# Between router and first expert group: another order of the first gather, of four identity products and of the overflow flag

## The reference

```
h = rms_norm(x, moe_norm_w)
gl = h @ w_rg + b_rg                       # group logits
gp = softmax(gl); gi = top_k(gl, 1)        # one group per token
el = (h @ w_re + b_re)[chosen group]       # 8 logits
top_v, top_i = top_k(el, 2); top_w = softmax(top_v) * g_w
comb = weight of each of 32 experts, zero for all but two
out = sum over experts e of
      (silu(h @ w_gate[e]) * (h @ w_up[e]) * comb[:, e]) @ w_down[e]
x = x + out
```

## Time and profile before

| | us |
|---|---|
| three runs: median (lowest to highest) | 846.97 (846.54 to 847.56) |
| profiled execution, its own time | 844.72 |
| its span, first to last instruction | 842.9 |
| mean granted TensorE clock, share of full | 0.966 |
| TensorE matmul busy | 760.5 (90%) |
| VectorE busy / ScalarE busy | 459.2 (54%) / 325.0 (39%) |
| moved by DMA | 190.25 MB, mean 226 GB/s |

### The profile page before, as it was taken

How to read it: one execution, slowest core, us unless ns; L and a number is a source line. 1 busy time by engine, 2 the same in 40 slices (tenths; PEclk the granted TensorE clock), 3 DMA queues, 4 the chain that set the end, 5 groups by cost and what they waited for, 6 DMA issues and landing times.

```text
span 842.9 us, 11017 instructions
## 1 busy us (share of the span) xinstructions
PE 760.5 (90%) x4618; PEld 573.6 (68%) x4618; DVE 459.2 (54%) x813; ACT 325.0 (39%) x482; POOL 17.8 (2%) x14
## 2 busy tenths in 40 slices
PE   4999999999999997988799896779999999999898
PEld 4978877788778875555445542337999865678676
DVE  5778955547756755132142121028687786754653
ACT  5555446535464423111011010037755541267521
POOL 0000000000000000000000000001100020000000
PEclk9999999999999997999899898789999999999999
DMA  9555543333467596699999999875463734243301
GB/s 317 172 199 199 200 150 101 100 101 101 149 244 277 191 425 260 213 422 420 421 421 420 419 422 391 338 265 185 146 228 94 255 130 149 101 150 100 100 1 51
DMA packets 62578, 190.25 MB, mean 226 GB/s; under 512 B 7417, under 2 KB 11771, under 8 KB 50044
## 3 DMA queue, kind: packets, MB, share of 16 engines
q1 hardware_dynamic: 60750, 184.70, 58.6%
q10 hardware_dynamic: 1774, 4.79, 1.8%
HBM read 188.43 MB, written 1.05 MB: 225 GB/s over the span
## 4 chain that ended last, share of the span: by engine, by line
PE 59%; DMA 16%; DVE 13%; ACT 8%; issue 2%; POOL 1%; SPq 0%; ACTq 0%; DVEq 0%; POOLq 0%
PE pb L500 56%; DMA raw<-in_w_exp_up 7%; DVE WL L1705 4%; DMA WHo<-in_w_exp_up 4%; ACT WH L1209 4%; PE pb L509 3%; DMA WLo<-in_w_exp_up 3%; DMA raw<-in_w_exp_gate 2%; ACT arena L1365 1%; DMA X<-in_x 1%; DVE cv_ L1811 1%; DVE arena L1970 1%; POOL small L2587 1%; ACT arena L1237 0%; DVE arena L2016 0%
## 5 line engine op out<-in xcount | busy, mean ns | idle before, releaser
L1705 DVE TENSOR_TENSOR WL<-raw,WH 128x2048 fp32r<-128x2048 f32 (+5 forms) x80 | 173.4, 2177 | 98.2 <-ACT WH L1209 98.1
L1209 ACT ACTIVATE WH<-raw 128x2048 fp32r<-128x2048 f32 (+5 forms) x80 | 144.9, 1822 | 99.4 <-PE pb L500 89.9
L500 PE MATMUL pb<-WH,HTh 128*128 128x512 f32 (+2 forms) x384 | 156.0, 406 | 13.6 <-DVE HTl L1735 3.4
L500 PE MATMUL pb<-WL,HTh 128*128 128x512 f32 (+2 forms) x384 | 148.3, 386 | 0.0
L500 PE MATMUL pb<-WH,HTl 128*128 128x512 f32 (+2 forms) x384 | 148.0, 386 | 0.0
L500 PEld LDWEIGHTS pb<-WH,HTh 128*128 128x128 f32 x384 | 72.7, 189 | 33.7 <-DVE WL L1705 6.4
L500 PEld LDWEIGHTS pb<-WL,HTh 128*128 128x128 f32 x384 | 72.5, 189 | 14.4
L500 PEld LDWEIGHTS pb<-WH,HTl 128*128 128x128 f32 x384 | 72.8, 190 | 12.9 <-issue 1.0
L500 PE MATMUL pb<-arena 128*32 128x256 f32 (+6 forms) x268 | 64.0, 466 | 7.4 <-DMA arena<-in_w_exp_up 4.8
L500 PE MATMUL pb<-WH,arenao 128*128 128x512 f32 x192 | 59.6, 392 | 1.2 <-DVE arenao L1739 1.2
L2244 DVE TENSOR_TENSOR rt_<-rt_,pb 128x256 f32<-128x256 f32 x8 | 3.4, 421 | 98.9 <-ACT rt_ L1480 98.9
(11 more groups left out here) (360 smaller groups left out, 1287.4 us busy)
## 6 DMA issues: line engine op xcount, KB each, us to landing
raw<-in_w_in SPq DMA_DIRECT2D x46, 1024.0 KB, 5.1
raw<-in_w_exp_up SPq DMA_DIRECT2D x16, 1024.0 KB, 21.3
arena<-in_w_exp_gate SPq DMA_DIRECT2D x14, 1024.0 KB, 19.1
WLo<-in_w_exp_down SPq DMA_DIRECT2D x11, 1024.0 KB, 17.0
raw<-in_w_exp_gate SPq DMA_DIRECT2D x10, 1024.0 KB, 14.8
WHo<-in_w_exp_down SPq DMA_DIRECT2D x9, 1024.0 KB, 16.5
raw<-in_w_out SPq DMA_DIRECT2D x8, 1024.0 KB, 5.1
arena<-in_w_exp_down SPq DMA_DIRECT2D x8, 1024.0 KB, 16.0
```

Source lines behind the costliest of these rows:

```text
L500: return e.matmul(o, l, r, start=start, stop=stop, skip_group_check=True)
L1209: e.activation(h_, r_, ACT.Copy).then_inc(hi.sem, hi.mark(k))
L1705: e.tensor_tensor(l_, r_, h_.bitcast(F32), ALU.subtract).then_inc(lo.sem, lo.mark(k))
```

## The change

Five edits, all between the router and the end of expert group 0.

- The seed of the first accumulator stands between the two halves of the router product, behind the transposes; the other three stay where they were.
- Two products `keep_warm` (identity with a quarter of X, into the bank of `xg` 0, which no one reads before the gather overwrites it) stand before and after `rank`.
- The first gather is `gather_first`: first the 16 matmuls with the high part, t = 0 and then t = 1, into all four banks; then the 16 with the low part, bank by bank. P is made in two instructions, one for each t, and the high part of t waits for its own half alone; only the low part waits for XNl.
- `first` waits chunk by chunk, for the engine that drains that chunk. VectorE drains the first gather before it works on `comb`, and `ranks(1)` stands ahead of the overflow.
- `over` and its two VectorE operations move behind `hidden_T` of group 0, ahead of the next gather. With it gone from the first gather, `first(0, ...)` takes the bank of `xg` 2, and the two banks that go round in group 0 are taken by gate/up, slots, hidden, over, xg(1,0), xg(1,1) in this order.

```
+            def seed(i):
+                held_acc.append(ring.take(("acc", i), (ac, ac, ve, ve)[i], at=where[("nm", "T", 2 * i)]))
+                mul(held_acc[i][:, :], ident, X[:, i // 2, 512 * (i % 2):512 * (i % 2) + 512], True, False).then_inc(
+                    mm.sem, mm.mark("x acc"))
...
                 if half == 0:
                     halves_T("nm", X, 1, ("x mix", 1))
+                    seed(0)
...
-            held_acc = [ring.take(("acc", i), (ac, ac, ve, ve)[i], at=acc[i]) for i in range(4)]
...
-            for i in range(4):
-                mul(held_acc[i][:, :], ident, X[:, i // 2, 512 * (i % 2):512 * (i % 2) + 512], True, False).then_inc(
-                    mm.sem, mm.mark("x acc"))
+            for i in (1, 2, 3):
+                seed(i)
             o = ring.take("rank", ve)
+            xg = [ring.take(("xg", 0, 0), ve)]
+            def keep_warm():
+                mul(xg[0][:, :], ident, X[:, 0, 0:512])
+            keep_warm()
             ve.wait_ge(e, "sel")
...
+            keep_warm()
+            def gather_first():
+                xg.extend(ring.take(("xg", 0, j), ve) for j in (1, 2, 3))
+                def part(x, t, c, start, stop):
+                    return mul(xg[c // 2][:, (c % 2) * 256:(c % 2) * 256 + 256], x[:, t, slice(c, c + 127 * 8 + 1, 8)],
+                               P[0][:, t, :, :].rearrange("p e l -> p (e l)"), start, stop)
+                ac.wait_ge(e, "xh")
+                for t in range(2):
+                    ve.wait_ge(e, ("P", 0, t))
+                    for c in range(8):
+                        part(XNh, t, c, t == 0 and c % 2 == 0, False)
+                for j in range(4):
+                    for t in range(2):
+                        ve.wait_ge(e, ("xl", t))
+                        for c in (2 * j, 2 * j + 1):
+                            ins = part(XNl, t, c, False, t == 1)
+                    ins.then_inc(mm.sem, mm.mark(("xg", 0, j)))
...
             def first(q, m):
...
-                for j in range(4):
-                    ac.wait_ge(e, ("xg", q // 2, j))
-                    ve.wait_ge(e, ("xg", q // 2, j))
                 for c in range(8):
+                    (ac, ve)[c % 2].wait_ge(e, ("xg", q // 2, c // 2))
...
-            for j in range(4):
-                gather(0, j)
-            o = ring.take("over", ve)
-            ve.wait_ge(e, "any")
-            mul(o[0:1, 0:1], any_, C["ones"][:, 0:1]).then_inc(mm.sem, mm.mark("over"))
+            gather_first()
...
                 hidden_T(q)
+                if q == 0:
+                    o = ring.take("over", ve)
+                    ve.wait_ge(e, "any")
+                    mul(o[0:1, 0:1], any_, C["ones"][:, 0:1]).then_inc(mm.sem, mm.mark("over"))
```

On VectorE:

```
             def ranks(q):
...
-                e.tensor_tensor(P[q % 2], sv, iv, ALU.is_equal).then_inc(ve.sem, ve.mark(("P", q)))
+                for t in range(2):
+                    sv = slot[:, t, 8 * q:8 * q + 8].unsqueeze(2).to_broadcast([128, 8, CAP])
+                    iv = iota.unsqueeze(1).to_broadcast([128, 8, CAP])
+                    e.tensor_tensor(P[q % 2][:, t, :, :], sv, iv, ALU.is_equal).then_inc(
+                        ve.sem, ve.mark(("P", q, t), ("P", q)))
...
             ranks(0)
             gather_low(1)
+            for j in range(4):
+                gather(0, j)
...
-            for j in range(4):
-                gather(0, j)
+            ranks(1)
             ve.wait_ge(e, "comb")
             e.scalar_tensor_tensor(out=over, in0=sel, scalar=CAP + 0.5, in1=comb, op0=ALU.is_gt, op1=ALU.mult)
-            mm.wait_ge(e, "over")
-            e.tensor_scalar(any_[0:1, :], pb("over")[0:1, 0:1], 1.0, None, ALU.min).then_inc(ve.sem, own("over"))
-            ve.wait_ge(e, "over")
-            e.tensor_copy(flag[0:1, :], any_[0:1, :]).then_inc(ve.sem, own("flag"))
-            ranks(1)
...
+                if q == 0:
+                    mm.wait_ge(e, "over")
+                    e.tensor_scalar(any_[0:1, :], pb("over")[0:1, 0:1], 1.0, None, ALU.min).then_inc(ve.sem, own("over"))
+                    ve.wait_ge(e, "over")
+                    e.tensor_copy(flag[0:1, :], any_[0:1, :]).then_inc(ve.sem, own("flag"))
```

More of the change, by code:

```diff
@@ L762, in tensor @@
             gemm_around(("wo", 1), MT, "mT", 4, lambda: halves_T("nm", X, 0, ("x mix", 0)))
+            held_acc = []
+            def seed(i):
+                held_acc.append(ring.take(("acc", i), (ac, ac, ve, ve)[i], at=where[("nm", "T", 2 * i)]))
+                mul(held_acc[i][:, :], ident, X[:, i // 2, 512 * (i % 2):512 * (i % 2) + 512], True, False).then_inc(
+                    mm.sem, mm.mark("x acc"))
             o = ring.take("lg", ac)
@@ L794, in gather @@
                 ve.wait_ge(e, ("P", q))
-                ve.wait_ge(e, ("xl", 0))
-                ve.wait_ge(e, ("xl", 1))
-                ac.wait_ge(e, "xh")
                 for c in (2 * j, 2 * j + 1):
@@ L2149, in ranks @@
                     mm.wait_ge(e, ("xg", q - 2, 3), ("pt", 2 * q - 3))
-                sv = slot[:, :, 8 * q:8 * q + 8].unsqueeze(3).to_broadcast([128, 2, 8, CAP])
-                iv = iota.unsqueeze(1).unsqueeze(1).to_broadcast([128, 2, 8, CAP])
-                e.tensor_tensor(P[q % 2], sv, iv, ALU.is_equal).then_inc(ve.sem, ve.mark(("P", q)))
+                for t in range(2):
[3 more added lines that the diff above has]
+                        ve.sem, ve.mark(("P", q, t), ("P", q)))
             def gather(q, j):
```

## The result

The changed kernel took 840.03 us (median of four, 839.53 to 840.62) against 847.13 (four, 846.54 to 847.56): 7.1 us less, ratio 0.9917, interval 0.9900 to 0.9934. The forecast was 844.0, 3.0 less, with a range down to 842.0. The direction was right and the size was not.

What follows compares the result with a forecast made beforehand. Up to down 0 the hand-overs between TensorE, ScalarE and VectorE, then a transfer stream to 524, bound it; -2.45 (order) + 0.31 (flag) - 0.86 (clock) = -3.0 from 846.97 gives 844.0, range 842.0 to 846.7.

Steps and rivals of the forecast that it cites:

- What bounds the kernel: From 354 to 524 an unbroken transfer stream at 417 GB/s, anchored at the end of down 0; before it, engine hand-overs.
- Seed 0, first product, second product: Around the router and `rank`: the moved seed and both unread products fit into waiting time, price 0 each.
- High parts first: Start of first gather: released by the half-size P at 323.79 in place of 325.28, a gain of 1.49 us.
- From gather to gate: Gate 0 follows bank 2's drains, starting at 331.85 in place of 334.30: 2.45 us gained, the 1.49 included.
- The gather itself: First gather: its 32 matmuls keep 7.95 us, 0.24 apart, at either clock.
- rival 4: Gather: the strided load is not the limit; 0.19 a matmul saves 1.6 us more, 842.4; chance 0.04.
- The flag: Next gather, behind up 0: its bank comes free later, so it starts 0.31 us later (bounds 0.2 to 0.6).
- The clock: Gate 0: half of the 1.7 us lost at half clock comes back, 0.86; down 0's loss stays as it is.
- lower end: Router to down 0: order, all 1.7 at gate 0 and 1.1 at down 0, -4.9 us in all, 842.0.
- From the stage to the end: Behind down 0: the gain made up to there was expected to arrive whole at the end.
- Rival 1: Through gate 0: products bring nothing, clock as before, only order counts; -2.1 us, 844.8; chance 0.17.
- Rivals 2, 3 and 5: 2: gate 0 low clock 6.8 us, 846.5, 0.10; 3: products delay router, 849.8, 0.08; 5: nothing arrives, 847.0, 0.05.

Runs made afterwards that it cites:

- the two kernels with early constants: ScalarE's transfers of the constants issued right behind SiLU of group 0: in the changed kernel 837.38 against 846.39, in the kernel before 844.51 against 846.48.
- the later medians: The changed kernel, unedited, on two further occasions against the kernel before: 841.39 against 846.39 us, and 841.74 against 846.48.
- the pooled medians: Medians over pooled executions without further edit: changed kernel 841.2 us (17 executions in three sets), kernel before 846.5 (77).

## Why the prediction was right or wrong

*What bounds the kernel:* right in kind, wrong in one point. The stage to 524 is a stream without a break, before and after. But it doesn't start at the end of down 0 alone. The constants' transfers, which ScalarE issues 4.6 us ahead of SyncE's issue in the kernel before and 3.6 ahead in the changed one, share it. That part of the gain is lost to them is my reading: 4.86 at SyncE's issue is 4.0 at the end of up 2 in the first profile. That they cost the stream about 2 us at up 2 is shown by the two kernels with early constants.

*Seed 0, first product, second product:* priced at 0 and found at 0; `rank` starts where it did, 10.26 from the residual sum.

*High parts first:* forecast 1.49, measured 1.41. *From gather to gate:* forecast 2.45 in all, measured 2.36, with bank 2's drain as the releaser. *The gather itself:* right, 7.95 forecast and 7.9 measured at full clock; the run without stride shows that the load sets the pace, so rival 4 is out as it was put. (That stride would cost nothing was my inference from the rule on the column count; the section named there says nothing of stride.) *VectorE's order:* 0, as put. *The flag:* forecast 0.31; from the end of up 0 to the next gather it is 2.23 for 1.90, 0.33.

*The clock:* this is the step that failed, a term of the sum that was sized too small. "I take half of the 1.7 back", and nothing at down 0. Measured: all 1.7 (up 0 ends 4.04 earlier, gate 0 started 2.36 earlier) and 1.06 at down 0 (4.76 to 3.70). That is 2.8 where the sum had 0.86, and -4.9 where it had -3.0; it was the lower end's own sum. I had argued that a gather which loads more than it multiplies might let the clock fall just before gate 0. The experiments show that the gather may let it fall, but early in it, and that it is back by gate 0 in every profile in which gate 0 follows closely: with products (7 of 7) and without (3 of 3). The products alone, with the microsecond of idling kept, get nothing. So the idle time before gate 0 was the thing to price, with the whole 1.7 hung on it. For the 1.06 at down 0 the runs show less: in the kernel before a fall lies over the end of the next gather and the first two steps of down 0; in the changed kernel there is none, or one that is over before down 0 starts. What moves it is open.

*From the stage to the end:* I took it as whole. From the residual sum to the end of the span the gain is 4.7, 4.0 and 1.8 in three profiles; 1.5 goes in the second block each time. So that the 4.9 at SyncE's issue and the 5.0 and 4.7 of the later medians are alike is in part luck, and no proof that the gain arrives whole.

*The comparison:* the forecast was to be read against a median of three. The place ahead of 311 that moves by 3 us from one execution to the next is not in the change and not in my range. Of the first set's 7.1 the stage accounts for 4.9; the other 2.2 are in no profile, and their cause stays open. Against the pooled medians the first set's kernel before is 0.6 high and its changed kernel 1.2 low, so most of the excess lies with the changed kernel. That the place ahead of 311 made both is likely and not shown: the four executions of the kernel before have no profile of their own, and of the changed kernel's four one has, without the fall.

Rival 1 was half right: the order does bring most, with or without the products, but not with the clock as before; without them up 0 ended 4.02 earlier, where rival 1 gives 2.45. Rivals 2, 3 and 5 did not come: no long low stretch stood in gate 0, the router was not delayed, and a gain arrived.

## What to carry to other kernels

Where an engine idles for a microsecond between two of its own stages, price the next stage's half clock with it, and look for the wait to shorten before adding work that only keeps the engine busy. Where a stage is a stream of transfers, look at what else is in the queues when it starts; small transfers that another engine issues there are moved into idle time for the price of one block of code. And where a few tenths of a per cent count, put profiles of two executions of one kernel side by side first: they show which stages move by themselves.

## What was not expected of the hardware

A weight load of 128 columns with a stride of 8 floats takes 336 ns and without it 191, and the 256-column matmuls of the gather are 0.24 us apart with the stride, at either clock, and 0.13 without it (32 in 4.1 us, at full clock). The Trainium skill, "TensorE: Matmul & The Clock Gate", section "Step-by-step: what each phase is for", has a load's time scale with the column count and not with the rows; both loads here have 128 columns and differ in the stride alone, so in this case the count does not settle the time by itself. ScalarE's copy of 128x1024 with the same stride in its source takes 2.1 us in place of 1.1. And the half clock at about 235 comes in six of fourteen profiles, though the code there is the same in all.
